# Interleaving the first two units of the entry, a second weight tile in two pieces, and the forget logits as four more columns of the values' matmuls

## The reference, cut to what matters

```
# first layer of the first block: the normed input times one wide matrix
xn = _rms_norm(h, norm_g[layer, 0])
gq, gk, gv, glr, gr, nq, kc, vc, ks, vs, kw, vw, ng = split(xn @ w_in)
# second block: another wide matrix, of which fz are 4 columns, one a head
z = h @ w_in
qa, ka, va, qb, kb, vb, fz, gza, gzb = split(z)
log_f = log_sigmoid(fz + b_forget)
F = cumsum(log_f, axis=1)              # over the 512 tokens
s = qb @ kb.T * scale + (F_q - F_k)    # scores of the forgetting attention
...
return rms_norm(x, norm_final)         # [512, 1024], the output
```

## Time and profile before

| what | value |
|---|---|
| median of 3 runs | 1991.33 us |
| time of the profiled execution | 1992.63 us |
| its span | 1990.9 us |
| PE, PEld busy | 99%, 83% |
| DVE, ACT, POOL busy | 51%, 35%, 20% |
| mean granted TensorE clock | 0.999 |

### The profile page before, as it was taken

The page is one execution under the profiler, slowest core; times in us unless marked ns, Lnnn a source line. Parts: engine busy times, 40 slices in busy tenths (PEclk is TensorE's granted clock), DMA queues, the critical chain, the costliest instruction groups (busy, mean ns, idle before and its releaser), DMA issues.

```text
span 1990.9 us, 27158 instructions
## 1 busy us (share of the span) xinstructions
PE 1973.5 (99%) x11044; PEld 1655.7 (83%) x11044; DVE 1018.7 (51%) x1391; ACT 695.1 (35%) x1008; POOL 406.8 (20%) x212
## 2 busy tenths in 40 slices
PE   8999999999999999999999999999999999999998
PEld 7878888888888888889888888888877888888887
DVE  5468757457345336626727535642544664322435
ACT  6357643122124323315312212534434352222222
POOL 1000007696600001000568661000000200000000
PEclk9999999999999999999999999999999999999999
DMA  6221134444333232222445442232221223323231
GB/s 190 79 64 44 44 117 148 158 149 147 129 106 117 73 108 85 85 102 91 156 138 169 148 134 100 85 94 81 71 85 64 86 84 106 104 98 106 84 106 64
DMA packets 135033, 208.91 MB, mean 105 GB/s; under 512 B 6347, under 2 KB 105865, under 8 KB 134921
## 3 DMA queue, kind: packets, MB, share of 16 engines
q1 hardware_dynamic: 125952, 180.37, 27.9%
q0 software_dynamic: 6912, 25.17, 3.8%
q10 hardware_dynamic: 2056, 1.76, 0.3%
HBM read 205.18 MB, written 2.10 MB: 104 GB/s over the span
## 4 chain that ended last, share of the span: by engine, by line
PE 94%; DVE 3%; ACT 2%; issue 0%; ACTq 0%
PE ps L2158 28%; PE ps L2160 28%; PE ps L2159 28%; PE ps L2219 1%; PE ps L2609 1%; PE ps L2212 1%; PE ps L2211 1%; PE ps L2620 1%; PE ps L2709 1%; PE ps L2182 1%; PE ps L2801 1%; DVE m L1466 0%; PE ps L2598 0%; PE ps L2597 0%; ACT ps L761 0%
## 5 line engine op out<-in xcount | busy, mean ns | idle before, releaser
L1388 DVE TENSOR_TENSOR w_lo<-w_raw,w_hi 128x2048 fp32r<-128x2048 f32 x149 | 350.9, 2355 | 577.0 <-ACT w_hi L726 577.0
L2158 PE MATMUL ps<-x_hi,w_hi 128*128 128x512 f32 x1240 | 489.1, 394 | 0.4 <-DVE w_lo L1388 0.4
L2160 PE MATMUL ps<-x_hi,w_lo 128*128 128x512 f32 x1240 | 483.0, 390 | 0.0
L2159 PE MATMUL ps<-x_lo,w_hi 128*128 128x512 f32 x1240 | 482.9, 389 | 0.0
L726 ACT ACTIVATE w_hi<-w_raw 128x2048 fp32r<-128x2048 f32 x151 | 288.9, 1913 | 536.1 <-PE ps L2160 435.1
L2158 PEld LDWEIGHTS ps<-x_hi,w_hi 128*128 128x128 f32 x1240 | 233.0, 188 | 51.0 <-issue 3.5
L2160 PEld LDWEIGHTS ps<-x_hi,w_lo 128*128 128x128 f32 x1240 | 232.7, 188 | 48.8
L2159 PEld LDWEIGHTS ps<-x_lo,w_hi 128*128 128x128 f32 x1240 | 233.1, 188 | 45.9
L2158 PE MATMUL ps<-w_hi,h_hi 128*128 128x512 f32 x688 | 267.8, 389 | 0.0
L2160 PE MATMUL ps<-w_hi,h_lo 128*128 128x512 f32 x688 | 267.7, 389 | 0.0
L2159 PE MATMUL ps<-w_lo,h_hi 128*128 128x512 f32 x688 | 267.7, 389 | 0.0
(11 more groups left out here) (404 smaller groups left out, 2694.2 us busy)
## 6 DMA issues: line engine op xcount, KB each, us to landing
w_raw<-in_ffn_w SPq DMA_DIRECT2D x64, 1024.0 KB, 5.4
ada_w<-in_w_ada POOLq DMA_DIRECT2D x48, 512.0 KB, 4.2
w_raw<-in_w_ffn_in SPq DMA_DIRECT2D x22, 1024.0 KB, 5.1
w_raw<-in_w_in SPq DMA_DIRECT2D x20, 1024.0 KB, 5.4
w_raw<-in_o_w_in SPq DMA_DIRECT2D x16, 1024.0 KB, 5.4
w_raw<-in_w_ffn_out SPq DMA_DIRECT2D x11, 1024.0 KB, 4.9
w_raw<-in_e_w_in SPq DMA_DIRECT2D x9, 1024.0 KB, 5.4
w_raw<-in_o_w_out SPq DMA_DIRECT2D x8, 1024.0 KB, 4.9
```

The source lines that it names most:

```text
L1388: nc.vector.tensor_tensor(w_lo[:, slot, :], w_raw[:, slot, :], w_hi[:, slot, :].bitcast(F32), ALU.subtract).then_inc(w_lo_ready, 1)
L2158: nc.tensor.matmul(dst, a_hi, b_hi, start=start, stop=False)
L2159: nc.tensor.matmul(dst, a_hi, b_lo, start=False, stop=False)
L2160: return nc.tensor.matmul(dst, a_lo, b_hi, start=False, stop=stop_)
```

## The change

At the entry, the small tile's lower 64 columns move: `w_lo` of the 64 columns that are used is written into the other 64 columns of `w_hi`, so that 16 matmuls give all of unit 0 (rows 0 to 63 of the result are the correction, which ACT moves and DVE adds). Units 0 and 1 are interleaved k by k (`first_two`), unit 1 one k behind. Tile 1 is loaded in two pieces of 128 columns; DVE rounds the first and ACT the second. The nine rows of constants are issued by SP behind tile 1. x tile 2 is scaled by ACT instead of DVE, x tile 3 is squared half by ACT and half by DVE, `warm(8)` becomes `warm(4)` and `warm(6)` moves from before tile 2 to before tile 1. POOL no longer makes a `w_lo`.

In the second block "s_small" is gone. Tile `s_vb` takes 260 columns instead of 256, the last four being the forget logits, as four units of 24 matmuls in place of two of 48. The four columns are kept as `f_cols`, transposed by PE in pair 4, biased by DVE in pair 4, go through ACT in pair 5 and DVE in pairs 6 and 7. At the end ACT issues the store of its own half and SP that of DVE's.

```diff
-    ("s_qk", 6, 2), ("s_va", 3, 2), ("s_small", 1, 1), ("s_qkb", 2, 2), ("s_vb", 1, 2),
+    ("s_qk", 6, 2), ("s_va", 3, 2), ("s_qkb", 2, 2), ("s_vb", 1, 4),
@@ class Filler
-    return 2 if self.units[j][1] == "up" else DK
+    return {"up": 2, "straight": 4}.get(self.units[j][1], DK)
@@ sync
+    load_e(0)
+    sp.dma_start(by8(w_raw, 1)[:, :, 0:P], w_e[:, :, GQ:GQ + P]).then_inc(w1_first, 16)
+    sp.dma_start(by8(w_raw, 1)[:, :, P:2 * P], w_e[:, :, GQ + P:GQ + 2 * P]).then_inc(w_loaded[1], 16)
+    row_load(0, 1, 8, A["norm_mix_2"][0].rearrange("(k p) -> k p", p=P))
...
+    for i in range(2, 4):
         load_e(i)
@@ vector, entry
+    square_x(1, slice(0, D), 0.0, 1)
     dve.wait_ge(consts_turned, 1)
     nc.vector.tensor_copy(cols[:, 0:32], ps[:, 0, 0:32]).then_inc(consts_taken, 1)
     normed(0, 0)
+    square_x(3, slice(D // 2, D), EPS, 15)
+    dve.wait_ge(squares, 3)
+    nc.vector.reciprocal(rstd[:, 2:3], root[:, 2:3]).then_inc(x2_rooted, 1)
     normed(1, 1)
-    square_x(3)
-    normed(2, 2)
-    normed(3, 3)
+    rooted(3)
...
+    dve.wait_ge(w_hi_ready, 1)
...
+    dve.wait_ge(w1_first, 16)
+    nc.vector.tensor_copy(by8(w_hi, 1)[:, :, 0:P], by8(w_raw, 1)[:, :, 0:P]).then_inc(w1_hi_half, 1)
     first_lo()
@@ vector, second block
     for pair in range(N_S // 2):
...
                 if pair == 1:
+                    forget_frame()
+                if pair == F_PAIR + 2:
                     forget_sum()
+                if pair == F_PAIR + 3:
+                    forget_rows()
@@ tensor, second block
+            def forget_turned():
+                pe.wait_ge(f_part, NT)
+                pe.wait_ge(a_normed, 2 * F_PAIR)
+                pe.wait_ge(a_taken, F_PAIR)
+                for t in range(NT):
+                    dst = ps[0:4, 4, (t + 1) * P:(t + 2) * P] if t < 3 else ps[0:4, 5, 2 * P:3 * P]
+                    o = nc.tensor.transpose(dst, f_cols[:, t, :], ident[:, :])
+                o.then_inc(f_turned, 1)
```

More of the change, by code:

```diff
@@ L433, in __init__ @@
                 self.steps = [(j, k) for j in range(len(self.units)) for k in range(self.depth(j))]
-                self.first = S["s_small"].unit
+                self.first = S["s_qkb"].unit
                 before, after = DK, (4, 4)
@@ L598, in _ @@
             load_rows("g_down1", w_g2, 12)
[L600 to L604, removed]
+            for t in range(3):
+                sp.wait_ge(final_done, t + 1)
+                sp.dma_start(out[0, t * P:(t + 1) * P, :], m[:, t, :]).then_inc(stored, 16)
+            sp.wait_ge(last_second, 1)
+            sp.dma_start(out[0, 3 * P:4 * P, D // 2:D], m[:, 3, D // 2:D]).then_inc(stored, 16)
+            sp.wait_ge(stored, 16 * 5)
         @block.gpsimd
@@ L725, in split_hi @@
                     act.wait_ge(mm_done, used)
-                nc.scalar.activation(w_hi[:, slot, :], w_raw[:, slot, :], ACT.Copy).then_inc(w_hi_ready, 1)
+                if isinstance(n, int) and n == S["s_vb"].first:
+                    nc.scalar.activation(w_hi_all[:, TILE:], w_raw_all[:, TILE:], ACT.Copy).then_inc(w_hi_ready, 1)
+                else:
+                    nc.scalar.activation(w_hi[:, slot, :], w_raw[:, slot, :], ACT.Copy).then_inc(w_hi_ready, 1)
             def split_next(st, i, q, it):
@@ L1240, in _ @@
             take_far(1)
-            nc.scalar.activation(root[:, 16:17], small[:, 22:23], ACT.Exp)
+            nc.scalar.activation(small[:, 23:24], small[:, 22:23], ACT.Exp)
             keep_far(3)
@@ L1293, in _ @@
             exp_scores(1)
-            n = S["s_small"].first + 1
+            n = S["s_qkb"].first + 1
             split_hi(n, n % 2, loaded(n), S["s_va"].done + 6)
@@ L1965, in forget_sum, with forget_rows @@
                                                         ALU.mult, ALU.add))
-                nc.vector.tensor_tensor(f_pick[:, :], ident[:, 0:4], ident[:, 32:36], ALU.add)
-                chain.link(nc.vector.tensor_scalar(f_two[:, :], causal_row[:, :], 0.0, None, ALU.mult))
+            def forget_rows():
+                fa = f_row[0:4, :]
                 chain.link(nc.vector.tensor_copy(f_two[0:4, :], fa))
@@ L1973, in split_closed @@
                     split_lo(filler.tile(j) + 2, filler.tile(j) % 2)
-            def forget_rest():
-                n = S["s_small"].first
-                hi, lo = by8(w_hi, n % 2), by8(w_lo, n % 2)
-                dve.wait_ge(w_lo_ready, n)
-                dve.wait_ge(w_hi_ready, n + 1)
-                chain.link(nc.vector.tensor_tensor(lo[:, :, 0:4], by8(w_raw, n % 2)[:, :, 0:4], hi[:, :, 0:4].bitcast(F32),
-                                                   ALU.subtract))
-                nc.vector.tensor_copy(hi[:, :, 32:36], lo[:, :, 0:4].bitcast(F32)).then_inc(w_lo_ready, 1)
             def split_half(n, part):
@@ L2419, in dense, with first_two @@
                             middle(x)
+                o.then_inc(mm_done, 1)
+            def first_two():
+                small_hi, gq_hi, gq_lo = by8(w_hi, 0), by8(w_hi, 1), by8(w_lo, 1)
+                pe.wait_ge(w_lo_ready, 1)
+                for k in range(DK + 1):
+                    if k == 1:
+                        pe.wait_ge(w1_hi_half, 1)
+                    if k < DK:
+                        pe.wait_ge(x_ready, k + 1)
+                        nc.tensor.matmul(ps[:, 0, :], small_hi[:, k, P:2 * P], x_hi[:, k, :], start=(k == 0), stop=False)
+                        o = nc.tensor.matmul(ps[:, 0, :], small_hi[:, k, P:2 * P], x_lo[:, k, :], start=False, stop=(k == DK - 1))
+                        if k == DK - 1:
+                            o.then_inc(mm_done, 1)
+                    if k:
+                        nc.tensor.matmul(ps[:, 1, :], gq_hi[:, k - 1, 0:P], x_hi[:, k - 1, :], start=(k == 1), stop=False)
+                        nc.tensor.matmul(ps[:, 1, :], gq_hi[:, k - 1, 0:P], x_lo[:, k - 1, :], start=False, stop=False)
+                pe.wait_ge(w1_lo_half, 1)
+                for k in range(DK):
+                    o = nc.tensor.matmul(ps[:, 1, :], gq_lo[:, k, 0:P], x_hi[:, k, :], start=False, stop=(k == DK - 1))
                 o.then_inc(mm_done, 1)
@@ L2879, in _ @@
             far_turn(3)
-            pe.wait_ge(bank_free, 4 + S["s_small"].unit)
+            pe.wait_ge(bank_free, 4 + S["s_qkb"].unit)
             s_scores(1)
```

205 lines of the change are left out of this document (117 added, 88 removed).

## The result

The changed kernel takes 2022.4 us (median of 4 runs, 2022.24 to 2023.2), the one before 1991.4 beside it: a ratio of 1.0155, 95% interval 1.0143 to 1.0167. It is 31 us slower, where 6 us faster was forecast. Its profiled execution has a span of 2020.7 us at a mean granted clock of 0.999.

The account below looks back on a forecast made before the run. PE bounds the kernel, with 94% of the chain that ended last. Terms -4.0 - 4.13 + 0.16 + 0.5 + 0.1 + 1.5 - 0.35 = -6.2 took the median 1991.33 to 1985.1 us, range 1983.0 to 1988.0.

Parts of the forecast that it names:

- the four new columns: Second block: 96 matmuls of 260 columns instead of 256 cost +0.16 us, or +10.3 if no better than 512 columns.
- Entry, -4.0: Start of kernel: first product 1.5 us earlier plus 2.5 us saved in the products of units 0 and 1.
- the earlier first product: Entry: first product at 15.55 us instead of 17.04, 1.5 us gained, between 0.9 and 1.7.
- the products themselves: Entry: units 0 and 1 take 40 matmuls instead of 48, 9.75 us instead of 12.25, 2.5 saved.
- rival 5: Start: PE falls to half its speed; all 40 matmuls at 1.2 GHz cost 9.1 us more, 1994.2 us; chance 0.03.
- Second block: Removing s_small and a w_lo wait gives -4.13 us; columns, transposes, emptying units and f_made add 0.16, 0.5, 0.1, 1.5.
- The wait for `f_made`: Second block, before pair 8's scores: PE waits for DVE's f_two, +1.5 us, ends 0.8 and 2.0.
- Rival 1: Second block: no wait for f_made, or it is found again in slack later; 1983.6 us; chance 0.13.
- The four transposes: Second block, pair 4: PE's transposes of the forget columns, 0.12 us each, +0.5, between 0.2 and 0.8.
- rival 3: Second block, pair 5: ACT late; if table changes cost double, PE waits 2.2 us, 1987.3 us; chance 0.05.
- rival 4: First layer: the entry's gain is lost again where something does not move with it; 1989.1 us; chance 0.07.
- End, -0.35: Last stores: DVE's half goes out at once, the other from ACT, last issue 0.4 us earlier; 0 to -0.7.

Follow-up runs that it names:

- run 12: Kernel before with only the changed kernel's allocations (w_raw, w_hi, w_lo of 2*TILE+32 columns, root of 16), same instructions: 2028.0 us, ratio 1.0182.
- run 1: Kernel before with root of 16 columns instead of 17, so tensors behind it start 32 bytes lower: 2033.3 us, ratio 1.0207.
- run 2: Kernel before with the three longer w tiles, root of 16 and neg_half in a column of small: 2019.5 us.
- run 4: Kernel before with an unused tensor of 64 bytes behind root: 2017.0 us.
- run 6: Kernel before with an unused tensor of 128 bytes behind root: 2030.6 us.
- run 9: Kernel before with an unused gap of 192 bytes behind root: 2021.4 us.
- run 10: TensorE alone, blocks of 48 matmuls with operands at given places: 11.10 to 11.15 us at equal places, 11.20 to 11.45 at others.
- run 14: Changed kernel, same instructions, laid out so large matmuls' operands stand as before within 256 bytes: 1986.3 us, ratio 0.9974 to the kernel before.
- run 8: Kernel before with an unused tensor of 128 bytes ahead of w_raw, moving w_hi, w_lo and the region together: 1991.5 us, ratio 0.9999.
- run 13: Kernel before with only the change's entry part and two tail edits, no tensor moved: 1988.35 us, ratio 0.9985.
- run 15: As run 14, with f_two written in pair 6 instead of pair 7: 1986.0 us, ratio 0.9969 to the kernel before.
- run 5: Changed kernel with neg_half and root in columns of small, the shared region at a multiple of 128 bytes: 2015.1 us.
- run 3: Changed kernel with neg_half in a column of small, at the same addresses as run 2: 2013.6 us.
- run 11: TensorE alone, blocks of 192 matmuls in the kernel's groups of three at given places: 0.2270 to 0.2336 us a matmul.

## Why the prediction was wrong

**The step that failed** is the sum itself, in what it takes as given: "from 0.120 for 256 and 0.227 for 512 a column costs 0.42 ns, so +0.16" costs the four new columns by what PE does with them, and the sum leaves all other matmuls at 0.227. That the tiles had to grow for these columns, and `root` to shrink for the tiles, was costed at nothing and not named. It was +36.3 us (run 12), the largest term by far. Runs 1, 2, 4, 6, 9 and 12 show that it needs no change of work, run 10 that TensorE alone has it and that, where both operands keep one place each, it goes by the difference of these places modulo 256, and run 14 that it vanishes when the difference is zero again. The slower matmuls are the large ones of every stage; those of 260 columns, whose rows have 1040 bytes and so go through many places, start every 0.12 us as the 256 did.

The other steps, in run 14, where no difference of places disturbs them:

- **Entry, -4.0: mis-sized, some 3.4.** Against the profiled execution of before, the column scores of the second block start at 1377.8 instead of 1381.6, -3.8, and the first product, forecast at 15.3 to 15.9, is at 15.47 in the changed kernel and 15.62 in run 14. But this execution of before had a late start, and the prediction took its sum from it and applied it to the median. Run 8 has the same instructions:

```profile
5.45 0.32 ACTq L852 DMA_DIRECT2D const_rows<-in_nsa_cmp_pos  x1
...
9.89 1.94 PE L2174 MATMUL ps<-ident,m 128*128 128x128 f32 x16 [0.22 <-DVE m L1416]
...
15.87 0.47 PE L2409 MATMUL ps<-x_hi,w_hi 128*128 128x512 f32 x1 [0.95 <-DVE x_lo L1422]
...
28.07 0.69 PE L2427 MATMUL ps<-f_row,w_gate 16*128 16x512 f32 x1
```

ACT is through with its issues at 5.77 there and at 6.95 in the earlier trace rows, and the first product follows 1.2 earlier, at 15.87. Over the nine traces with the old entry the first product lies between 15.68 and 17.04 (median 16.14) and the gate scores between 27.92 and 29.22 (28.48); over the six with the new one between 14.87 and 15.62 (15.30) and between 24.76 and 25.43 (25.09). So, as an estimate from these traces, the earlier first product is worth about 0.8, forecast 1.5, and the products themselves 2.4 in run 14 against run 8, forecast 2.5. With 0.3 for the tail this lies near run 13's 3.3 and within its interval.

In run 15's profiled execution 1.4 of the gain is lost again where the granted clock was 0.82 and 0.97, and run 5's has 0.72 from 25 to 30 us, and is 1.4 slower than the other three executions of its kernel; the nine traces with the old entry show 1.00 there. This is rival 5 in small: part of a stretch at the lower of the two levels, not 40 matmuls.
- **Second block.** From the column scores to `yt_hi` it is 168.6 us instead of 170.7: -2.1, against -4.13 + 0.16 + 0.5 + 0.1 + 1.5 = -1.87. The wait for `f_made` was 1.4 in the changed kernel and in run 14, forecast 1.5, at the place that was named. Rival 1 is out. The four transposes start 0.11 apart, and the next matmul 0.53 behind the first of them, forecast 0.5.
- **ACT in pair 5 (rival 3).** No run shows PE waiting for ACT there; the only such row is the 0.2 us on `n_prob` in the first layer. The two table loads of that pair take 1.28 us each in run 14, at 1442.66 and 1444.61, and the next operation starts 0.01 behind each, so no drain shows there either.
- **First layer (rival 4).** No new wait. Against the profiled execution of before the gate scores came 3.8 earlier, and so did the second block.
- **End, -0.35.** The last of the `mg_hi` matmuls and the end are 5.9 and 6.2 us earlier in run 14 than before: -0.3 for the tail.
- **Sum.** -6.2 was forecast; in three layouts the change gave -5.4, -5.6 and -5.8 (runs 14, 12 and 3). By the traces it is -3.4 - 2.1 - 0.3 = -5.8; what is missing against the forecast is in the entry.

The Trainium skill (SBUF — State Buffer, SBUF: two separate sides) says that on the side of the engines only the port pair shared by VectorE and GpSimd makes anyone wait, "PE, ACT, and DVE's dedicated pair never wait on anyone", and its table there gives TensorE a second, independent read port for the weights. Run 10 disagrees: with every other engine idle, the place of the stationary operand against the moving one makes 48 matmuls take 11.10 or 11.41 us. The measurement decides: the pace of a matmul depends on where its two operands stand to each other, so the two reads are not independent in their effect on the time. By what mechanism was not found.

What stays open: in the changed kernel matmuls of one kind, with the same operands, run in groups of three of 0.693 us in one stretch and of 0.700 in another: w moving against `h2` takes 0.693 from 356 to 421 us and 0.700 from 490 to 555. What sets which one was not found. Run 11 gave one level to each of its blocks. Where the places within a group differ, the difference is not the whole rule either: w at 0, 128, 0 moving against 128 took 0.2292 us in run 11, where two matmuls at run 10's 0.2324 for a difference of 128 and one at 0.2267 would give 0.2305. Why a difference of 64 to one side costs a third of one to the other was not found either.

## What to carry to other kernels

Before costing a change by its instructions, compare the addresses of every operand of the hot matmuls, modulo 256, before and after: a tensor that grows or shrinks anywhere ahead of them moves all that follow, and here that cost six times what the work gained. Keep stationary and moving operands at the same place modulo 256, with each long-lived tensor a multiple of 256 bytes long and the small odd ones at the end or as columns of one tensor. When a trace shows a busy PE, no new wait and a granted clock of 1.00, and the time still differs, count the matmuls of an untouched stretch.

## What the hardware showed that was not expected

- A matmul of 512 columns of this type starts every 0.2267 us when both operands lie at one place modulo 256, every 0.229 us when the stationary one lies 64 bytes behind (with the exception in run 9), and every 0.231 to 0.234 us at the other differences measured here.
- With 256 columns there is no such loss (5.97 us for 48 at difference 0, 5.91 at 128).
- Stationary operands of different places spoil the pace of those that match: w at 0, 0, 128 under x at 128 gave 0.2336 as the mean of all three (run 11), and sta 0 and 128 in turn under mov 0 took 11.36 us, where sta 0 alone took 11.15 and 128 alone 11.38 (run 10).
